# First weight chunks of layer 0, modulation sums and window gathers moved to other places of a two-block transformer kernel

## The reference

```python
def even_mixer(t, layer_idx, w_in, ...):              # first mixer, layer 0
    proj = t @ w_in                                   # 1024 x 2560
    y_a = diff_attention(proj[..., :3 * DIFF_WIDTH], ...)
    y_b = conformer_conv(proj[..., 3 * DIFF_WIDTH:], ...)
    return concatenate([y_a, y_b]) @ w_out

def conformer_conv(g, dw_w, ...):
    u = g[..., :CONV_CHANNELS] * sigmoid(g[..., CONV_CHANNELS:])
    y = conv_general_dilated(u, dw_w, ...)            # depthwise, 31 taps
    ...
def swiglu(h, w_gate, w_up, w_down):
    return (silu(h @ w_gate) * (h @ w_up)) @ w_down

# second block
silu_c = silu(c)
mod = silu_c @ w_mod[l] + b_mod[l]                    # shifts, scales and gates of layer l
h = rms_norm(x, norm1[l]) * (1 + sc1) + sh1
... = split(h @ w_in[l], ...)
ya = na_latent(qa, ka, va, ka_c, va_c, bias, row_idx) # windows of 16 columns; values gathered by window
yb = gqa_latent(...)
x = x + g1 * branch_merge(ya, yb, ...)
x = x + g2 * swiglu_2(rms_norm(x, norm2[l]) * (1 + sc2) + sh2, ...)
```

## Time and profile before

| | |
|---|---|
| runs | 1868.39, 1863.65, 1863.73 us |
| median | 1863.73 us |
| the profiled execution, its own time | 1853.85 us |
| its span in the trace | 1851.7 us |
| PE busy | 1790.0 us, 97% of the span |
| POOL busy | 1379.2 us, 74% |
| ACT busy | 905.8 us, 49% |
| DVE busy | 752.3 us, 41% |

### The profile page before, as it was taken

How to read it: one execution, slowest core, us unless ns; L and a number is a source line. 1 busy time by engine, 2 the same in 40 slices (tenths; PEclk the granted TensorE clock), 3 DMA queues, 4 the chain that set the end, 5 groups by cost and what they waited for, 6 DMA issues and landing times.

```text
span 1851.7 us, 28968 instructions
## 1 busy us (share of the span) xinstructions
PE 1790.0 (97%) x9894; PEld 1445.8 (78%) x9894; DVE 752.3 (41%) x1421; ACT 905.8 (49%) x1410; POOL 1379.2 (74%) x813
## 2 busy tenths in 40 slices
PE   8989999999899999999999999999999999999997
PEld 6667888766688888777888887778888977778886
DVE  3364332484455564353111555441114655441112
ACT  5346434444644454555344545654345445654443
POOL 6438999348798869568888884578887894578884
PEclk9999999999999999999999999999999999999999
DMA  7886566488787836435665463346664563346561
GB/s 244 241 284 221 184 202 209 156 278 297 257 269 257 262 124 187 133 120 184 202 198 184 157 188 110 114 150 202 195 190 155 164 185 124 113 149 189 186 191 70
DMA packets 255124, 348.26 MB, mean 188 GB/s; under 512 B 21176, under 2 KB 153400, under 8 KB 255032
## 3 DMA queue, kind: packets, MB, share of 16 engines
q1 hardware_dynamic: 252624, 341.49, 57.8%
q10 hardware_dynamic: 2408, 5.57, 1.0%
HBM read 343.24 MB, written 1.64 MB: 186 GB/s over the span
## 4 chain that ended last, share of the span: by engine, by line
PE 83%; DVE 6%; POOL 4%; ACT 3%; DMA 2%; issue 1%; SPq 1%; DVEq 0%; ACTq 0%; POOLq 0%
PE bank L2350 22%; PE bank L2352 22%; PE bank L2351 22%; PE bank L2458 2%; POOL wl L766 2%; POOL wl L765 2%; PE bank L3043 2%; PE bank L3033 1%; PE bank L2424 1%; PE bank L3082 1%; PE bank L2394 1%; PE bank L2393 1%; PE bank L2392 1%; DMA raw<-in_l_w_in 1%; PE bank L2700 1%
## 5 line engine op out<-in xcount | busy, mean ns | idle before, releaser
L806 POOL TENSOR_TENSOR wl<-raw,wh 128x1024 fp32r<-128x1024 f32 x300 | 734.0, 2458 | 110.1 <-ACT wh L998 83.8
L2350 PE MATMUL bank<-wh,xh 128*128 128x512 f32 (+2 forms) x1614 | 636.4, 394 | 18.0 <-POOL wl L766 10.3
L2352 PE MATMUL bank<-wl,xh 128*128 128x512 f32 (+2 forms) x1614 | 622.0, 385 | 0.0
L2351 PE MATMUL bank<-wh,xl 128*128 128x512 f32 (+2 forms) x1614 | 620.4, 384 | 0.0
L765 POOL TENSOR_TENSOR wl<-raw,wh 128x512 fp32r<-128x512 f32 (+2 forms) x234 | 312.8, 1337 | 304.1 <-ACT wh L833 304.1
L998 ACT ACTIVATE wh<-raw 128x1024 fp32r<-128x1024 f32 x270 | 286.6, 1063 | 434.7 <-PE bank L2352 421.1
L2350 PEld LDWEIGHTS bank<-wh,xh 128*128 128x128 f32 x1614 | 304.4, 189 | 85.8 <-issue 15.0
L833 ACT ACTIVATE wh<-raw 128x1024 fp32r<-128x1024 f32 (+2 forms) x268 | 276.5, 1052 | 183.3 <-PE bank L2352 101.6
L2352 PEld LDWEIGHTS bank<-wl,xh 128*128 128x128 f32 x1614 | 303.8, 188 | 62.2
L2351 PEld LDWEIGHTS bank<-wh,xl 128*128 128x128 f32 x1614 | 304.8, 189 | 55.9
L766 POOL TENSOR_TENSOR wl<-raw,wh 128x512 fp32r<-128x512 f32 (+2 forms) x234 | 313.5, 1340 | 0.0
(11 more groups left out here) (390 smaller groups left out, 1977.2 us busy)
## 6 DMA issues: line engine op xcount, KB each, us to landing
raw<-in_w_ffn_in SPq DMA_DIRECT2D x264, 256.0 KB, 2.9
raw<-in_w_in SPq DMA_DIRECT2D x224, 256.0 KB, 2.9
raw<-in_w_mod SPq DMA_DIRECT2D x152, 256.0 KB, 4.3
raw<-in_w_ffn_out SPq DMA_DIRECT2D x132, 256.0 KB, 2.9
raw<-in_l_w_gate SPq DMA_DIRECT2D x88, 256.0 KB, 3.7
raw<-in_l_w_up SPq DMA_DIRECT2D x88, 256.0 KB, 4.5
raw<-in_l_w_down SPq DMA_DIRECT2D x88, 256.0 KB, 3.6
raw<-in_l_w_in SPq DMA_DIRECT2D x48, 256.0 KB, 4.6
```

Of the source, the lines that this page charges most:

```text
L806: nc.gpsimd.tensor_tensor(wl[:, s, :], raw[:, s, :], words(wh)[:, s, :], ALU.subtract)\
L2350: mm(dst, x_hi, w_hi, start=first, stop=False, skip_group_check=True)
L2351: mm(dst, x_lo, w_hi, start=False, stop=False, skip_group_check=True)
L2352: return mm(dst, x_hi, w_lo, start=False, stop=last, skip_group_check=True)
```

## The change

Four things at the start. `FIRST_LOWS` becomes 6, so that DVE computes half of the low part of chunks 4 and 5 as well, and whoever waits for the low part of these waits for both engines. ACT copies chunk 5 ahead of the roots, and Silu of `c` goes behind the two Sigmoids. SP issues the constants behind chunk 5 and the row vectors and gains behind chunk 7. DVE's row reductions, tap mask and tap products go behind `u0`; the definitions of helpers between the two places (`reduced`, `angles`, `discretise`, `state_tables`, `rotate`) stand elsewhere in the file, but are called where they were.

In ffn0 and ffn1 `mod_turn` comes after the first chunk of step 1, not after the third. In x0 and x1 the sixteen gathers stand ahead of the load of the last chunk of tile `PRELUDE + 1`, three chunks sooner in SP's list. The bodies of the moved definitions are cut from the diff.

```diff
@@ -295,7 +295,7 @@
-    FIRST_LOWS = 4
+    FIRST_LOWS = 6
@@ -717,7 +717,7 @@
                     for j in range(plan.first[name], plan.end(name)):
-                        if name in ("in_x0", "in_x1") and j == plan.tiles[name][PRELUDE + 2][2][2][0]:
+                        if name in ("in_x0", "in_x1") and j == plan.tiles[name][PRELUDE + 1][2][3][0]:
                             sp.wait_ge(evac, plan.tile_no[name] + PRELUDE)
                             for g, first_col in enumerate(WINDOWS):
                                 for r in range(4):
@@ -726,8 +726,9 @@
                         load(j)
                         if j == 1:
                             load_x(slice(D // 2, D), x_in1)
-                        if j == 3:
+                        if j == 5:
                             sp.dma_start(con[:, P:], a["consts"][:, P:]).then_inc(con_in, 16)
+                        if j == 7:
                             sp.dma_start(row[:, :], a["rows"].broadcast_to([P, NR])).then_inc(row_in, 16)
                             sp.dma_start(gain[:, :], a["post"][0:1, :].broadcast_to([P, D])).then_inc(gain_in, 16)
@@ -1034,9 +1035,8 @@
             norm_high("mix0", "l0_mix_pre", (3,))
-            hi_until(5)
+            hi_until(6)
             norm_roots("mix0", X, x_loaded)
-            nc.scalar.activation(csilu, V_("c"), ACT.Silu).then_inc(c_silu, 1)
             act.wait_ge(con_in, 16)
@@ -1047,6 +1047,8 @@
             for t, b in enumerate(pair_of("in0", 1)):
                 nc.scalar.activation(g0[:, t, :], b[:, :], ACT.Sigmoid, scale=back[:, t:t + 1]).then_inc(glu_sig, 1)
+            nc.scalar.activation(csilu, V_("c"), ACT.Silu).then_inc(c_silu, 1)
+
@@ -1602,10 +1604,130 @@
             for j in range(FIRST_LOWS):
-                norm_low("mix0", "l0_mix_pre", (j,))
+                if j < 4:
+                    norm_low("mix0", "l0_mix_pre", (j,))
                 low_half(j)
             norm_backs("mix0")
...
+            dve.wait_ge(con_in, 16)
+            tile_done("in0", 0)
+            for t, b in enumerate(pair_of("in0", 0)):
+                dve.wait_ge(glu_sig, t + 1)
+                v.scalar_tensor_tensor(out=u0[:, t, :], in0=b[:, :], scalar=back[:, t:t + 1], in1=g0[:, t, :], op0=ALU.mult,
+                                       op1=ALU.mult).then_inc(glu_done, 1)
+            dve.wait_ge(glu_done, 2)
+            v.engine_nop().then_inc(evac, 2)
             dve.wait_ge(row_in, 16)
             for i, (q, k) in enumerate((("lq1", "lk1"), ("lq2", "lk2"))):
...
                 v.tensor_tensor(tap_w[:, n], spread(tap_mask[:, :].unsqueeze(1), 4 * TAP_GROUPS, 32),
                                 spread(w[:, n], 4 * TAP_GROUPS, 32), ALU.mult).then_inc(tap_set, 1)
...
-            dve.wait_ge(con_in, 16)
-            tile_done("in0", 0)
-            for t, b in enumerate(pair_of("in0", 0)):
-                dve.wait_ge(glu_sig, t + 1)
-                v.scalar_tensor_tensor(out=u0[:, t, :], in0=b[:, :], scalar=back[:, t:t + 1], in1=g0[:, t, :], op0=ALU.mult,
-                                       op1=ALU.mult).then_inc(glu_done, 1)
-            dve.wait_ge(glu_done, 2)
-            v.engine_nop().then_inc(evac, 2)
@@ -2583,8 +2587,9 @@
                 j1 = j0 + GU_CH
                 ahead_of_turn = GU_CH - 1 if name in UNDIVIDED else GU_CH // 2
-                gate_up(j1, step=1, chunks=range(ahead_of_turn))
+                gate_up(j1, step=1, chunks=range(1))
                 between()
+                gate_up(j1, step=1, chunks=range(1, ahead_of_turn))
                 hidden_turn()
```

More of the change, by code:

```diff
@@ L1608, in _ @@
             step(v.tensor_scalar(back_q, back, float(DH) ** -0.5, None, ALU.mult))
[L1609 to L1622, removed]
             def reduced(x, turns, count):
@@ L1741, in _ @@
             v.engine_nop().then_inc(evac, 2)
+            dve.wait_ge(row_in, 16)
+            for i, (q, k) in enumerate((("lq1", "lk1"), ("lq2", "lk2"))):
+                v.tensor_tensor_reduce(R_(q), R_(q), R_(k), 1.0, 0.0, ALU.mult, ALU.add, lamp[:, i:i + 1]).then_inc(lam_p, 1)
+            dve.wait_ge(c_silu, 1)
+            v.tensor_copy(cw[:, :, 22:24], csilu.rearrange("p (k s) -> p k s", s=2)).then_inc(c_set, 1)
+            dve.wait_ge(ident_in, 16)
+            step(v.tensor_reduce(tap_mask[:, :], ident.rearrange("p (j c) -> p c j", c=32), AX_X, ALU.add))
+            settle()
+            w = V_("dw_w").unsqueeze(2)
+            for c in range(CONV_T):
+                n = slice(4 * TAP_GROUPS * c, 4 * TAP_GROUPS * c + 4 * TAP_GROUPS)
+                v.tensor_tensor(tap_w[:, n], spread(tap_mask[:, :].unsqueeze(1), 4 * TAP_GROUPS, 32),
+                                spread(w[:, n], 4 * TAP_GROUPS, 32), ALU.mult).then_inc(tap_set, 1)
             def take_rotated(i, lo, scale):
```

## The result

| | before | changed |
|---|---|---|
| median of 12 runs | 1863.69 us | 1846.65 us |
| lowest to highest | 1850.97 to 1868.39 | 1845.27 to 1858.36 |
| the profiled execution | 1853.85 | 1846.03 |

The ratio is 0.9922 (95% interval 0.9902 to 0.9942): faster, and by more than forecast. The medians are 17.0 us apart, the two profiled executions only 7.8, close to the 6.6 of the sum. Both kernels have single executions some 10 to 12 us longer than the rest: before above 1860, here 7 of 12; changed above 1854, here 3 of 12. That is the main matter of this document.

What follows compares the result with a forecast made beforehand. It took TensorE's own work, 83% of the span, as the bound, so only PE stalls could be won. Terms of −6.63 from 1853.85 gave 1847.2, plus the 9.9 to the median 1857.1 us; range 1852 to 1864.

Steps and rivals of the forecast that it cites:

- the sum: All five places added, −5.27 − 1.42 + 0 + 1.46 − 1.40 = −6.63 us, taken from the profiled execution.
- the last of the sum: The profiled execution's 9.9 us below the runs' median was carried over, turning 1847.2 into 1857.1 us.
- Start: Behind chunk 4, PE's wait of 3.59 us and 1.67 of slow clock both go: −5.27 us.
- full blocking: At the start, tap products hold POOL for their whole 7.87 us, a half up to 3.26: 1861.9 us, chance 0.06.
- ffn0: At the first hidden block's turn, moving the modulation sums two chunks sooner removes PE's stall: −1.42 us.
- ffn1: At the same turn, the 1.46 us won is waited at the next turn instead, 2.2 there: 0 us.
- the first rival: New waits in ffn1 and x0 may each draw a slow-clock stretch of 1.67 us: 1858.8 to 1860.5, chance 0.18.
- x0: Ahead of the window values, load 7 behind the gathers delays PE's transposes and nothing is won: +1.46 us.
- x1: Window values start at 1524.25 instead of 1525.65, the wait for the gather gone but transposes later: −1.40 us.
- the third rival: In x0 and x1, load 7 lands late behind the gathers: up to 1875.1 us, middle 1869.4, chance 0.12.
- the second sign of being wrong: In x0 and x1, the splits of fill chunk 7 wait beyond 1107 and 1522 us.
- the first, a new wait over 1 us ahead of 60: At the start, a new wait over 1 us before 60 us would show the prediction wrong.

Runs made afterwards that it cites:

- e1: The kernel before, unchanged, against itself: median 1855.76 us, ratio 0.9996; its traced execution was a long one, 1866.39 us.
- e3: Only the modulation sums' place in ffn0 and ffn1 changed, against the kernel before: median 1853.75 us, ratio 1.0001; its traced execution took 1866.99.
- the waits: POOL waits in c0 ahead of splitting chunks 13 and 17 until DVE's head norm is done: kernel before 1853.61 us, changed kernel 1847.13 us.
- e2: Only the start changed, against the kernel before: median 1848.83 us, ratio 0.9968; it has times only, no trace used.
- e15: The changed kernel run once more, unchanged: median 1848.11 us, 1 of 12 runs long.
- e4: Only the place of the sixteen gathers in x0 and x1 changed, against the kernel before: median 1855.61 us, ratio 1.0019.
- e7: The kernel before plus two waits of POOL in c0 for DVE's head norm: median 1853.61 us, ratio 0.9947.
- e11: The changed kernel with POOL's two waits in c0, ffn1's modulation sums and x0's gathers back in their old places: median 1841.83 us, ratio 0.9914.
- e14: The kernel before with DVE taking the reciprocal ahead of c0's head norm three times: median 1866.66 us, 11 of 12 runs long.
- e8: The kernel before with one edit, ACT copying chunk 5 ahead of the roots: median 1852.16 us, ratio 0.9941.

## Why the prediction was wrong

The step that failed is the last of the sum: "That execution lies 9.9 us below the median of the runs, 1863.73; I carry the difference over". The difference was no constant. The profiled execution, 1853.85, was a short one; the three runs (1863.65 to 1868.39) were all long. A long one has a stall of some 12 us in c0 that the trace I priced did not contain. (The three have no trace; the two traced executions of before's start at that length, e1's and e3's, have the stall, and with the waits it and the long runs are gone.) The changed kernel's executions are mostly short, so its median lies at its own profiled execution: 1847.2 was worked out for that, 1846.03 was profiled and 1846.65 measured. That the changed kernel stalls less often was in no term of the sum, and why it does is open.

Point by point:

- **Start**, −5.27: right, with −5.5 between the traces and 5.0 between the medians of e2 and before. Nothing came late next: the tap products made four halves longer by 1.0 each and PE did not notice. (The 22.2 for the end of chunk 5 is worked out nowhere; the terms above it give 21.9 to 22.9, and the trace has 21.6.) I had read the 2.25 us of a half beside a tap as partial blocking, since full blocking came out at 3.26; but the 1.97 us of a product in that estimate were taken beside POOL, with the product's own waiting in them. The long executions show blocking of the whole instruction; four halves beside four products, 2.28 for 1.29, fit the two taking turns.
- **ffn0**, −1.42: right (−1.4).
- **ffn1**, 0, with a wait of 2.2 and perhaps a slow stretch as the first rival: both came, with +2.1 between the two traces. The wait is 2.6, and a stretch at 0.50 followed in six of the seven traces with that move (not in e15). But five of the nine traces without it have one there too, behind the 1.46 (e1, e4, e7, e11, e14), and the trace that I priced is one of the other four, so the longer wait is not shown to draw it. From 479.07 to 530.08 in before, ffn1 takes 51.0 to 52.1 us without the move and 51.8 to 53.2 with it, 1.3 apart in the mean.
- **x0**, +1.46: right (+1.55). **x1**, −1.40: −0.8. The text's own terms give −1.0: 1518.9 + 0.43 + 3.1 is 1522.4, not 1522.0. The rest is load 7. A chunk's load is two transfers, and the later one landed 3.0 us after its issue in x0 and 4.0 in x1, the direction of the third rival at a fraction of its price. (The old wait for the gather, 2.8 to 3.5 us, was followed by a stretch at 0.50 in three of the seven traces that have it, e3, e8 and e14, so taking it away is worth more than 0.8 in some executions.) Counted from DVE's evacuation, its split waited 0.4 us longer than forecast in x0 and 0.7 in x1, so the second sign of being wrong came; the first, a new wait over 1 us ahead of 60, did not.
- **Bounds.** The sum was within 1.2 us of what the profiled executions differ by, and within 0.2 of what the medians differ by once POOL waits in both kernels. That is in part luck: its five places measured −4.05 between the traces, and slow stretches that were absent by chance made up the rest. The range failed because it held the uncertain prices and not the 9.9 us, the largest unexplained number in the text. More than the whole expected gain stood between the trace and the median, and no rival asked where it was.

## What to carry to other kernels

Ahead of any sum, set the profiled execution against the spread of the runs: where they differ by more than the change is worth, the median has something in it that the trace hasn't, and a profile of another execution of the same kernel can show it. An instruction of DVE with two SBUF inputs that the critical path needs was not safe here beside a GpSimd engine that never pauses; two waits of 0.9 us on GpSimd at the right boundaries took away a stall of 12. And a gain found as an idle wait is real only if what is queued behind the moved work is not waiting for a transfer that lands at the same time as before (ffn1, x0).

## What was not expected of the hardware

One DVE product took 0.81 us alone, 1.36 beside GpSimd when it got its turn, and 27.5 when it lost 21 times in a row to GpSimd's next instruction; whether it is let in differs between executions of one kernel and between jobs (long in 4 of 35 runs in one, in 20 of 26 in another), and 0.6 us more of work ahead of it raised the share from 9 of 29 to 11 of 12.
